# High and low weight blocks placed 32 bytes further on in SBUF

## The reference

```python
def swiglu_ffn(h, g, w_in, w_out):
    gate, up = jnp.split(rmsnorm(h, g) @ w_in, 2, axis=-1)
    return (jax.nn.silu(gate) * up) @ w_out

for layer in range(DEPTH):                       # DEPTH = 2
    h = h + 0.5 * swiglu_ffn(h, ffn1...)
    hn = rmsnorm(h, mix_g)
    y = retention_mixer(hn, ...) if layer == 0 else fox_mixer(hn, ...)
    h = h + y
    h = h + 0.5 * swiglu_ffn(h, ffn2...)
    # after layer 0 also: k, v, logf = fox_kv(h, ...)
```

## The kernel before, in words

| buffer | before | remainder by 128 |
|---|---|---|
| xh | 34,944 | 0 |
| xl | 53,376 | 0 |
| raw | 71,808 | 0 |
| wh | 96,384 | 0 |
| wl | 108,672 | 0 |
| rstd | 120,960 | 0 |
| sTh | 123,360 | 96 |
| const | 130,272 | 96 |
| acth, actl | 138,816 and 166,464 | 64 |
| vtok, sTl (region ret) | 157,248 and 172,608 | 64 |
| ogh, ogl | 177,984 and 187,200 | 64 |
| foxh, foxl | 194,880 and 208,704 | 64 |

## Time and profile before

### The profile page before, as it was taken

The page is one execution under the profiler, slowest core; times in us unless marked ns, Lnnn a source line. Parts: engine busy times, 40 slices in busy tenths (PEclk is TensorE's granted clock), DMA queues, the critical chain, the costliest instruction groups (busy, mean ns, idle before and its releaser), DMA issues.

```text
span 2559.5 us, 44070 instructions
## 1 busy us (share of the span) xinstructions
PE 2528.0 (99%) x18791; PEld 2458.5 (96%) x18791; DVE 1054.6 (41%) x1556; ACT 697.3 (27%) x994; POOL 338.6 (13%) x266
## 2 busy tenths in 40 slices
PE   8999999999999999999999999999999999999998
PEld 8999999989898989999999999999998789999998
DVE  4332334554545555332334343323335754332333
ACT  4221222121312232221222232212223542221221
POOL 0100113210111103100113211100121021100112
PEclk9999999999999999999999999999999999999999
DMA  5232232222223122232232442322324322232231
GB/s 151 82 103 62 83 95 83 83 79 67 87 67 94 55 71 85 88 106 59 82 95 72 140 113 82 98 75 75 91 82 117 114 76 79 82 107 58 83 96 48
DMA packets 394197, 221.71 MB, mean 87 GB/s; under 512 B 8592, under 2 KB 386544, under 8 KB 394064
## 3 DMA queue, kind: packets, MB, share of 16 engines
q1 hardware_dynamic: 389328, 205.22, 27.8%
q0 software_dynamic: 4544, 14.50, 1.7%
q10 hardware_dynamic: 192, 0.04, 0.0%
HBM read 206.01 MB, written 13.71 MB: 86 GB/s over the span
## 4 chain that ended last, share of the span: by engine, by line
PE 96%; DVE 2%; ACT 1%; DMA 0%; issue 0%; SPq 0%; POOL 0%; ACTq 0%; DVEq 0%; POOLq 0%
PE ps L1536 88%; PE ps L1914 1%; PE ps L1719 1%; PE ps L1705 1%; PE ps L1707 1%; PE ps L1706 1%; PE ps L1942 1%; PE ps L1966 1%; DVE wl L602 0%; PE ps L1819 0%; PE ps L1698 0%; DVE xl L917 0%; PE ps L1739 0%; ACT wh L597 0%; DMA xtok<-in_x_sample 0%; PE ps L1778 0%
## 5 line engine op out<-in xcount | busy, mean ns | idle before, releaser
L602 DVE TENSOR_TENSOR wl<-raw,wh 128x1024 fp32r<-128x1024 f32 (+3 forms) x352 | 446.6, 1269 | 1269.3 <-ACT wh L597 1268.9
L1536 PE MATMUL ps<-xh,wl 128*128 128x288 f32 x4000 | 861.0, 297 | 5.9 <-DVE xl L917 4.1
L1536 PE MATMUL ps<-xl,wh 128*128 128x288 f32 x4000 | 852.7, 295 | 0.0
L1536 PE MATMUL ps<-xh,wh 128*128 128x288 f32 x4000 | 852.6, 295 | 0.0
L597 ACT CAST wh<-raw 128x1024 fp32r<-128x1024 f32 (+3 forms) x352 | 375.8, 1068 | 1154.8 <-PE ps L1536 1153.6
L1536 PEld LDWEIGHTS ps<-xh,wl 128*128 128x128 f32 x4000 | 642.1, 189 | 11.9 <-DVE xl L917 4.8
L1536 PEld LDWEIGHTS ps<-xh,wh 128*128 128x128 f32 x4000 | 642.7, 189 | 0.0
L1536 PEld LDWEIGHTS ps<-xl,wh 128*128 128x128 f32 x4000 | 642.7, 189 | 0.0
L1536 PE MATMUL ps<-actl,wh 128*128 128x288 f32 x1408 | 301.1, 295 | 0.0
L1536 PE MATMUL ps<-acth,wl 128*128 128x288 f32 x1408 | 300.9, 295 | 0.0
L1536 PE MATMUL ps<-acth,wh 128*128 128x288 f32 x1408 | 299.0, 294 | 0.0
(11 more groups left out here) (247 smaller groups left out, 1641.6 us busy)
## 6 DMA issues: line engine op xcount, KB each, us to landing
raw<-in_ffn_w_in SPq DMA_DIRECT2D x176, 512.0 KB, 3.8
raw<-in_ffn_w_out SPq DMA_DIRECT2D x32, 768.0 KB, 4.8
raw<-in_ret_w_in SPq DMA_DIRECT2D x48, 512.0 KB, 3.9
raw<-in_ffn_w_out SPq DMA_DIRECT2D x32, 640.0 KB, 4.4
raw<-in_ret_w_out SPq DMA_DIRECT2D x32, 256.0 KB, 2.8
raw<-in_fox_w_kvf SPq DMA_DIRECT2D x16, 512.0 KB, 4.1
raw<-in_fox_w_q SPq DMA_DIRECT2D x8, 512.0 KB, 4.9
bias<-cum_scratch SPq DMA_DIRECT2D x16, 256.0 KB, 3.5
```

What stands on the lines that cost most here:

```text
L602: nc.vector.tensor_tensor(wl[:, s % SPLIT, 0:kt, :], raw[:, s, 0:kt, :], wh[:, s % SPLIT, 0:kt, :].bitcast(F32), ALU.subtract).then_inc(lo ...
L1536: mm = nc.tensor.matmul(out[:, a:z], w, x[:, a:z], start=start and n == 0, stop=stop and n == len(terms) - 1)
```

## The change

Before wh is placed, the offset of the region "fixed" is moved on by 32 bytes, and behind wl by 96 more. So wh and wl lie 32 bytes further on, and every buffer behind them (rstd and all later ones, and the regions that begin where "fixed" ends) lies 128 bytes further on, which leaves its remainder by 128 as it was. h, xh, xl and raw stay where they are. No instruction, wait or transfer is added, removed or moved in order.

```diff
             raw_tails.append(sb("tails", f"raw_tail{s}", [P, (KMAX - KD) * P], F32R))
+        place["fixed"] += 32
         wh = sb("fixed", "wh", [P, SPLIT, KMAX, P], F32R)
         wl = sb("fixed", "wl", [P, SPLIT, KMAX, P], F32R)
+        place["fixed"] += 96
         rstd = sb("fixed", "rstd", [P, T])
```

## The result

The changed kernel takes 2583.95 us (median, 2583.48 to 2584.46) against 2562.44 for the kernel before, a ratio of 1.0084 with a 95% interval of [1.0072, 1.0097]. That is 21.5 us, outside the stated range of 2538 to 2579. The profiled execution took 2584.37 us with a span of 2582.7, against 2561.19 and 2559.5: 23.2 us more.

What follows compares the result with a forecast made beforehand. TensorE was taken as the bound, matmul count times pitch. All four steps summed to 0 us on the profiled 2561.19, put on the median as 2562.4 us, with a range of 2538 to 2579.

Steps and rivals of the forecast that it cites:

- What bounds the kernel: TensorE, busy 2528.0 of 2559.5 us; time is the number of matmuls times the pitch from start to start.
- The reading of the earlier trace: Pitch of the weight-block product by windows: xh/xl streams 133.3 ns dense or 130 quick, acth/actl streams 132.
- slower rival: Shifted weight block collides in quick sections, which fall to 133.3 ns: 12.7 us, 2575; with acth/actl 5.5 more, 2581; chance 0.27.
- Step 1: Weight loads of the main product (16,224, 188 ns) from the new place: 0 ns per load, pitch bounds 130 to 133.3.
- Step 2: ScalarE casts into wh, -8 to 0 ns; VectorE subtractions into wl, -38 to 0 ns; hidden behind TensorE, 0 us.
- Step 3: Spare tails of wh and wl as moving operand of 72 retention-product matmuls: at most 0.24 us, taken as 0.
- Step 4: Later buffers (rstd, acth and others) 128 bytes further on, remainder by 128 kept: 0 us.

Runs made afterwards that it cites:

- e4: All buffers, moving tiles and weight blocks alike, 32 bytes further on than in the kernel before; 2561.77 us, ratio 0.9994.
- e1: Against the kernel before, wh and wl stay and only the buffers behind them lie 128 bytes further on; 2567.38 us, ratio 1.0019.
- e6: Against the kernel before, wl alone 32 bytes further on, wh in place, buffers behind wl 128 on; 2563.85 us, ratio 1.0006.
- e3: Against the kernel before, wh and wl 96 bytes further on, the buffers behind them 128; 2583.91 us, ratio 1.008.
- e14: The change's two lines plus columns cut in 272 and 304 instead of 288 and 288, against the kernel before; 2582.87 us, ratio 1.0082.
- e2: Against the kernel before, wh and wl 64 bytes further on, the buffers behind them 128; 2562.04 us, ratio 0.9998.
- e8: Against the kernel before, wh and wl in place, all buffers behind them 64 bytes further on (acth at distance 0); median 2581.44 us, ratio 1.0077.
- e5: Against the kernel before, wh alone 32 bytes further on, wl and the buffers behind it 128 on; 2566.91 us, ratio 1.0018.
- e9: Kernel before with all buffers in place, columns cut in 272 and 304 instead of 288 and 288; 2561.77 us, ratio 0.9995.
- e10: Kernel before with buffers in place, columns cut in 256 and 320 instead of 288 and 288; 2574.52 us, ratio 1.0051.
- e12: Kernel before with the buffers behind wl 64 bytes further on and columns cut in 304 and 272, longer stream first; 2572.41 us, ratio 1.0041.
- e11: Kernel before with the buffers behind wl 64 bytes further on and columns cut in 272 and 304; 2554.66 us, ratio 0.9973.

## Why the prediction was wrong

- **What bounds the kernel** was right. TensorE's chain is the time, and a change in pitch goes straight into it: some 20 us of the difference are pitch.
- **The reading of the earlier trace rows** was a little off. The windows reach across the ends of sections: 184:259 holds 10 us of a quick section, so acth's level is 132.2 and not 131.8, and 260:384 ends with 10 us of acth, so the quick level is 130.0 and not 130.3. The slower rival's term for acth, 4,224 x 1.3 = 5.5 us, is 4,224 x 1.1 = 4.6 us by this.
- **Step 1 failed.** It took 0 ns per load because loads from a place 32 beyond a multiple of 64 take 188 ns, and because 512-column streams start 0.23 us apart beside them. Both are true after as well (188 ns, and 0.23 us between starts) and neither says what it was taken for. The cost is not in the load's duration, which is hidden; it is in the start of the next 288-column matmul. The step named the right guide itself, "the pitch levels are the only guide", and then chose the middle of its bounds, 0, for lack of a sign. In hindsight a sign was to be had from the earlier trace rows with the places in the table ahead of them: two distances, 0 and 64, had two kinds of level under one line, and the distance was about to become one that no row shows. The prediction noted that "the operands' places may take part" and yet costed the weights' place alone, where e4 shows that this place costs nothing by itself.
- **Step 2 held**: 1,048 and 1,249 ns are now 1,048 and 1,248, and 619 and 716 are 620 and 716. The gain to -38 ns that sTl's row left possible did not come.
- **Step 3** is not separated from the rest by any run. The largest group of its matmuls has a median of 394 ns, where it was 395; 72 matmuls can't carry more than a fraction of a microsecond in either case.
- **Step 4 was 5 us off in e1**, and e6, which has the same shift, is 1.6 us slower. Its argument on the pitch was right in the profiled execution of e1, where the levels stayed, though two sections exchanged theirs. What it left out is open: the granted clock, on which no row stood, accounts for the profiled execution and not for the median.
- **The slower rival is what happened**: quick sections fall to the dense level and acth with them, 18.2 us in its own working and 2581 us, with some 20 us of pitch measured, and the clock added. Its reason was the place ("both on multiples of 128, the most regular case, and any other can be worse"); with everything 32 bytes off such a multiple nothing is lost (e4). It had 0.27. The range ended at 2579, below the rival's own upper figure; the bound of that case should have been its end, 2581, and some room above.
- **The rule of the Trainium skill**, that a weight load takes no read bandwidth from the running matmul ("TensorE: Matmul & The Clock Gate", the part "What happens when you issue a matmul"), gave exactly 0. These runs don't agree with what was drawn from it: the pitch follows the distance between the two operands (e4 against the change, 2562 against 2584 us at the same place of the weights).

**What is shown and what is not.** Shown: with both weight blocks at a distance of 32 or 96 from the moving tiles, all 288-column streams run at 133.3 ns (the change, e3; e14 for another cut); at 64 they run at 132.2 (acth before, xh with e2), at 0 at 130.0 or 133.3 (xh before, acth with e2 and e8), whatever the place itself (e4). Not shown: by what path in the chip, why distance 0 has two levels and what picks one, by what rule mixtures of distances or of lengths combine (e5, e6, e9, e10, e12), and what makes the clock fall once in one trace and three or four times in another.

## What to carry to other kernels

Where TensorE streams back to back, the places of the two operands relative to each other are a parameter of the kernel, though no instruction shows it: count matmuls per window for each pair of tiles, with both ends of a window inside one section, and set the counts beside the byte distance of the pair by 128. In this kernel the distances 32 and 96 were the worst (133.3 ns everywhere), 64 was steady at 132.2, and 0 was either the best or as bad as 32: with all tiles at 0, three executions of e8 took 2581.3 to 2582.5 us, hardly less than the change. So an equal remainder is not a safe rule; measure each. When a buffer is put in or taken out ahead of one of the operands, a change like the 0.84% here can come that has nothing to do with what the buffer is for. To tell a cost of place from one of distance, move everything together once, as e4 does.

## What the runs showed of the hardware that was not expected

- One stream of 288 float32r columns beside a weight load has levels of 130.0, 132.2 and 133.3 ns between starts, set by the distance of the operands; with both blocks at 32 or 96 it was 133.3 in every section, never more. With one block at 32 or 96 there are two more, 131.9 (e6) and 132.6 (e5).
- At distance 0 two levels, 130.0 and 133.3, hold for whole sections of some 1,000 matmuls, and may differ between executions of one program (e8: 2572.33 and 2581.3 to 2582.5 us).
- Cutting the columns in 272 and 304 removes the two levels: 131.7 ns with 272 columns at distance 0 and 304 at 64, and 132.7 with 304 at 0 and 272 at 64, in either order. That is 2554.66 (e11) against 2572.41 us (e12) for the same work. With 256 and 320 columns distance 0 is at 133.3 throughout and distance 64 at 131.65 (e10).
- The granted clock falls more often in some executions than in others with the same instructions: the profiled execution of e1 lost 7.0 us by it and that of before 1.6 (0.85 and 0.91 in windows of 20 us, mean clock 0.995 against 0.998). So the clock is to be looked at window by window where two profiled executions differ by 0.2% and their pitches agree. A difference of medians is laid to it only where the clocks of the timed executions differ too; those of e1 and of before do not (0.9963 and 0.9964).
